# A token mixer on one core: pooling ahead of the attention, and six output projections split in two halves by their contraction

## The reference, cut to what matters

```python
def token_mixer(h, cos, sin, w_in, w_pool, pool_scale, sinks, g_pool, g_attn, w_out):
    z = h @ w_in
    u = z[..., :POOL_WIDTH]
    q = z[..., POOL_WIDTH:MIX_WIDTH].reshape(B, S, N_HEADS_2, HEAD_DIM_2)
    ...
    pool_out = pool_mix(u, w_pool, pool_scale)
    q = apply_partial_rope(q, cos, sin)
    k = apply_partial_rope(k, cos, sin)
    attn_out = swa_with_sinks(q, k, v, sinks)
    y = jnp.concatenate([rms_norm_2(pool_out, g_pool), rms_norm_2(attn_out, g_attn)], axis=-1)
    return y @ w_out
```

## Time and profile before

| | us |
|---|---|
| median of three executions | 2226.62 |
| lowest, highest | 2226.55, 2234.54 |
| the profiled execution, its whole time | 2232.97 |
| its span, first to last instruction | 2231.1 |
| TensorE busy in the span (97%) | 2171.8 |
| VectorE busy (56%) | 1258.4 |
| ScalarE busy (37%) | 819.9 |
| GpSimd busy (9%) | 194.2 |
| mean granted TensorE clock | 0.988 |

### The profile page before, as it was taken

One profiled execution on the slowest core, in us unless ns is written; L12 is line 12 of the kernel. 1 busy time (PEld: TensorE's weight loads), 2 busy tenths in 40 slices (PEclk: granted clock), 3 DMA queues, 4 the chain that ended last, 5 costly groups with the idle time before them and its releaser, 6 DMA issues.

```text
span 2231.1 us, 34854 instructions
## 1 busy us (share of the span) xinstructions
PE 2171.8 (97%) x14232; PEld 1811.3 (81%) x14232; DVE 1258.4 (56%) x1889; ACT 819.9 (37%) x1256; POOL 194.2 (9%) x142
## 2 busy tenths in 40 slices
PE   6999999999999999999999999999999899999998
PEld 5878788788888888888888888888897589888887
DVE  4789988898755555444533554443247735444423
ACT  4344433345454333223322542322233544322222
POOL 0100222103323001000000100000000210000000
PEclk9999999999999999999999999999999999999999
DMA  4242111122112243233332322333221112223321
GB/s 161 78 132 76 58 44 44 54 76 63 40 39 77 86 149 121 94 97 100 106 104 73 114 76 94 96 100 114 96 66 57 38 57 76 94 94 98 118 92 51
DMA packets 56170, 189.88 MB, mean 85 GB/s; under 512 B 6256, under 2 KB 8688, under 8 KB 56048
## 3 DMA queue, kind: packets, MB, share of 16 engines
q1 hardware_dynamic: 53168, 182.88, 25.3%
q10 hardware_dynamic: 2880, 5.24, 0.6%
HBM read 178.66 MB, written 9.44 MB: 84 GB/s over the span
## 4 chain that ended last, share of the span: by engine, by line
PE 81%; issue 10%; DVE 7%; ACT 2%; POOL 0%; DMA 0%; SPq 0%; ACTq 0%; DVEq 0%; POOLq 0%
PE pg L654 68%; PE pC L917 4%; PE pB L917 1%; DVE cpad L1883 1%; DVE sacc L2024 1%; DVE w_lo L1803 1%; PE pB L685 1%; ACT w_hi L1225 1%; PE pC L758 1%; PE pA L977 1%; PE pA L732 0%; PE pB L692 0%; PE pB L716 0%; PE pC L732 0%; DVE tb L2148 0%
## 5 line engine op out<-in xcount | busy, mean ns | idle before, releaser
L654 PE MATMUL pg<-a_hi,w_hi 128*128 128x512 f32 (+1 forms) x1920 | 747.2, 389 | 11.9 <-ACT ptile L1315 3.2
L654 PE MATMUL pg<-a_lo,w_hi 128*128 128x512 f32 (+1 forms) x1920 | 740.1, 385 | 0.0
L654 PE MATMUL pg<-a_hi,w_lo 128*128 128x512 f32 (+1 forms) x1920 | 737.8, 384 | 0.0
L1803 DVE TENSOR_TENSOR w_lo<-w_raw,w_hi 128x1024 fp32r<-128x1024 f32 (+3 forms) x299 | 382.6, 1280 | 395.3 <-ACT w_hi L1225 392.9
L1225 ACT ACTIVATE w_hi<-w_raw 128x1024 fp32r<-128x1024 f32 (+3 forms) x299 | 329.6, 1102 | 648.1 <-PE pg L654 637.1
L654 PEld LDWEIGHTS pg<-a_hi,w_hi 128*128 128x128 f32 x1920 | 362.7, 189 | 86.1 <-issue 8.0
L654 PEld LDWEIGHTS pg<-a_hi,w_lo 128*128 128x128 f32 x1920 | 362.8, 189 | 68.6 <-issue 1.6
L654 PEld LDWEIGHTS pg<-a_lo,w_hi 128*128 128x128 f32 x1920 | 362.9, 189 | 68.1 <-issue 0.9
L654 PE MATMUL pg<-h_hi,w_hi 128*128 128x512 f32 (+1 forms) x572 | 215.7, 377 | 0.6 <-DVE w_lo L1803 0.6
L654 PE MATMUL pg<-h_hi,w_lo 128*128 128x512 f32 (+1 forms) x572 | 214.5, 375 | 0.0
L654 PE MATMUL pg<-h_lo,w_hi 128*128 128x512 f32 (+1 forms) x572 | 212.4, 371 | 0.0
(11 more groups left out here) (359 smaller groups left out, 2346.7 us busy)
## 6 DMA issues: line engine op xcount, KB each, us to landing
w_raw<-in_w_gu SPq DMA_DIRECT2D x132, 512.0 KB, 3.5
w_raw<-in_w_in SPq DMA_DIRECT2D x74, 512.0 KB, 3.5
w_raw<-in_w_dn SPq DMA_DIRECT2D x48, 704.0 KB, 4.0
spill_g<-tmp ACTq DMA_DIRECT2D x16, 256.0 KB, 2.0
w_raw<-in_w_co SPq DMA_DIRECT2D x8, 512.0 KB, 3.6
w_raw<-in_w_do SPq DMA_DIRECT2D x8, 512.0 KB, 3.7
w_raw<-in_w_wo SPq DMA_DIRECT2D x8, 512.0 KB, 4.1
w_raw<-in_w_pg SPq DMA_DIRECT2D x8, 512.0 KB, 4.1
```

Source lines behind the costliest of these rows:

```text
L654: ins = pe.matmul(dst[:, cols], w_of(w, n % 2, k), b(k)[:, cols], start=first and q == 0, stop=last and q == len(todo) - 1)
L1803: dve.tensor_tensor(w_lo[:, n % 2, 0:c], w_raw[:, n % 4, 0:c], w_hi[:, n % 2, 0:c].bitcast(F32), ALU.subtract).then_inc(S("w_lo"), 1)
```

## The change

The weight of the six first output units is loaded in two halves: `mp` t, over the four pooling tiles, and `ma` t, over the four attention tiles, 12 products each. The mixer's input units stand in another order: `mu` 3 to 0 ahead of `mq` 0 and 1, all six whole ahead of the attention, with the four pooling matmuls between. The pooling part's norm (6) is summed in step 0 and spread in step 1; its factor goes to `tmp2`, its four tiles are scaled in steps 3 to 6 and their low parts taken in steps 7 to 10. Fillers are now `mq` 2 and 3 (8 products in each of three steps, none in steps 3 and 7), then `mp` 0 to 3: 3 products in each of steps 8 to 15, 8 in steps 16 to 18. `mp` 4 and 5 stand around the second norm (7). ScalarE copies an `mp` to `wd` or `up`; VectorE adds it to the `ma` of the same t on its way to `hb2`, ScalarE squares `hb2`. The factor `mix_post` moves from ScalarE's copy to VectorE's update of x. `mo` 6 and 7 stay whole.

```diff
@@ -315,3 +315,6 @@
-        MIX = [("mk", 0), ("mv", 0), ("mq", 0), ("mq", 1), ("mq", 2), ("mu", 3), ("mq", 3),
-               ("mu", 2), ("mu", 1), ("mu", 0)]
-        MFILL = MIX[5:]
+        MIX = [("mk", 0), ("mv", 0), ("mu", 3), ("mu", 2), ("mu", 1), ("mu", 0), ("mq", 0), ("mq", 1),
+               ("mq", 2), ("mq", 3)]
+        HALF_K = KT // 2
+        MFILL = [(("mq", 2), 3 * KT), (("mq", 3), 3 * KT)] + [(("mp", t), 3 * HALF_K) for t in range(4)]
+        MSTEP = [8, 8, 8, 0] * 2 + [3] * 8 + [8] * 3
+        assert sum(MSTEP) == sum(n for _, n in MFILL)
@@ -326 +329,4 @@
-        for i in range(KT):
+        for nm, k0 in (("mp", 0), ("ma", HALF_K)):
+            for i in range(KT - 2):
+                U.add((nm, i), a["w_out2"][i][:, k0 * P:(k0 + HALF_K) * P], HALF_K * P)
+        for i in range(KT - 2, KT):
...
+        MAUX = {3: 3, 7: 4}
+        YP = {("mu", 1): 3, ("mu", 0): 2, ("mq", 0): 1, ("mq", 1): 0}
+        for key in MIX:
@@ -399,4 +401,9 @@
-            for k in MAUX.get(3 * i + 2, []):
-                aux(k, "D" if k[0] == "rp" else "A")
-        aux(("yp", 0), "A")
-        for i in range(KT):
+            if key in YP:
+                aux(("yp", YP[key]), "A")
+            if key in (("mq", 2), ("mq", 3)):
+                aux(("rp", key[1] + 1), "D")
+        for i in range(KT - 2):
+            O.add(("mp", i), "A")
+        for i in range(KT - 2):
+            O.add(("ma", i), "D")
+        for i in range(KT - 2, KT):
...
+            def half_unit(key, k0, part=None):
+
+                n = U.at[key]
+                if part is None or part[0] == 0:
+                    pe.wait_ge(S("w_lo"), n + 1)
+                    begin(key)
+                ins = products(n, act_a(k0), HALF_K, bank(key), w_tile, part, ready=("a_lo", set_count("out", k0)))
+                if part is None or part[1] == 3 * HALF_K:
+                    ins.then_inc(S("gemm"), 1)
+
...
-            unit(("mq", 0))
-            unit(("mq", 1), part=(0, NORM_AT))
+            unit(("mu", 3), part=(0, NORM_AT))
@@ -1149,2 +1181,9 @@
-            unit(("mq", 1), part=(NORM_AT, UNIT))
-            unit(("mq", 2), part=(0, NORM_AT))
+            unit(("mu", 3), part=(NORM_AT, UNIT))
+            unit(("mu", 2))
+            unit(("mu", 1))
+            pooled(3)
+            unit(("mu", 0))
+            pooled(2)
+            unit(("mq", 0))
+            pooled(1)
+            unit(("mq", 1), part=(0, NORM_AT))
@@ -1152 +1191,2 @@
-            unit(("mq", 2), part=(NORM_AT, UNIT))
+            pooled(0)
+            unit(("mq", 1), part=(NORM_AT, UNIT))
...
@@ -1197,2 +1239,5 @@
-                if s < 15:
-                    unit(MFILL[s // 3], part=(s % 3 * UNIT // 3, (s % 3 + 1) * UNIT // 3))
+                for key, q, e, n in mixer_parts(s):
+                    if key[0] == "mq":
+                        unit(key, part=(q, e))
+                    else:
+                        half_unit(key, 0, (q, e))
@@ -1201,3 +1246,5 @@
-                for k in MAUX.get(s, []):
-                    (rotate if k[0] == "rp" else pooled)(k[1])
-            pooled(0)
+                    norm(6)
+                if s == 1:
+                    norm_out(6)
+                if s in MAUX:
+                    rotate(MAUX[s])
@@ -1205,2 +1252 @@
-            norm(6)
-            norm_out(6)
+            half_unit(("mp", 4), 0, (0, 8))
@@ -1207,0 +1254,2 @@
+            half_unit(("mp", 4), 0, (8, 12))
+            half_unit(("mp", 5), 0, (0, 4))
@@ -1208,0 +1257 @@
+            half_unit(("mp", 5), 0, (4, 12))
@@ -1210 +1259 @@
-                unit(("mo", t), ready=None if t else fresh("out"))
+                half_unit(("ma", t), HALF_K)
...
-            after(("mq", 1))
-            after(("mq", 2))
+            for key in MIX[2:8]:
+                if key == ("mq", 1):
+                    pooled(0)
+                after(key)
+                if key in YP and key != ("mq", 1):
+                    pooled(YP[key])
...
+            def pool_half(t):
+                after(("mp", t))
+                act.activation(pool_out(t), bank(("mp", t)), ACT.Copy).then_inc(S("evA"), 1)
+
+            def high_out(t):
+                act.wait_ge(S("mh"), t + 1)
+                act.activation(a_hi[:, t], mo[:, t], ACT.Copy).then_inc(S("a_hi"), 1)
@@ -1748,13 +1808,18 @@
-                if s < 15 and s % 3 == 2:
-                    after(MFILL[s // 3])
-                for k in MAUX.get(s, []):
-                    if k[0] == "yp":
-                        pooled(k[1])
-            pooled(0)
-            root(6)
-            for i in range(PT_):
-                act.wait_ge(S("oat"), i + 1)
-                square(7, i, mo[:, PT_ + i])
-            for t in range(PT_):
-                act.wait_ge(S("mh"), t + 1)
-                act.activation(a_hi[:, t], mo[:, t], ACT.Copy).then_inc(S("a_hi"), 1)
+                for key in mixer_done(s - 1) if s else []:
+                    if key[0] == "mp":
+                        pool_half(key[1])
+                    else:
+                        after(key)
+                if s == 0:
+                    root(6)
+                if 7 <= s < 7 + PT_:
+                    high_out(s - 7)
+                if s in (7, 11, 15):
+                    i = (s - 7) // 4
+                    act.wait_ge(S("oat"), i + 1)
+                    square(7, i, mo[:, PT_ + i])
+                if s == 15:
+                    act.activation(ost[:, 0:1], ost[:, 0:1], ACT.Sqrt)
+            act.wait_ge(S("oat"), PT_)
+            square(7, PT_ - 1, mo[:, KT - 1])
+            pool_half(3)
...
+            pool_half(4)
+            high_out(PT_)
+            high_out(PT_ + 1)
+            pool_half(5)
+            high_out(PT_ + 2)
+            high_out(PT_ + 3)
@@ -1766,4 +1834,3 @@
-                unit_out(act, ("mo", t))
-                full_square(2, t, bank(("mo", t)))
-                act.activation(hb2[:, t], bank(("mo", t)), ACT.Copy, scale=v("mix_post", t)).then_inc(S("evA"), 1)
-                after(("mo", t))
+                after(("ma", t))
+                ev_wait(act, ("ma", t))
+                full_square(2, t, hb2[:, t])
@@ -1774 +1841 @@
...
@@ -1841 +1908,2 @@
-                                ins = dve.scalar_tensor_tensor(y, src[:, t, TOK[h]], factor, y, ALU.mult, ALU.add)
+                                c = factor if isinstance(factor, float) else v(factor, t)
+                                ins = dve.scalar_tensor_tensor(y, src[:, t, TOK[h]], c, y, ALU.mult, ALU.add)
...
+            mixed(("mu", 3))
+            mixed(("mu", 2))
+            means(3)
+            mixed(("mu", 1))
+            means(2)
+            mixed(("mu", 0))
+            means(1)
+            mixed(("mq", 0))
+            means(0)
...
@@ -2493,10 +2573,14 @@
-                if s < 15 and s % 3 == 2:
-                    key = MFILL[s // 3]
-                    evac(key, zq[:, 1 + key[1]] if key[0] == "mq" else up[:, key[1], PW:])
-                if s % 3 == 0 and 0 < s < 16:
-                    after(MFILL[s // 3 - 1])
-                for k in MAUX.get(s, []):
-                    if k[0] == "rp":
-                        rotated(k[1])
-                if s in MEANS:
-                    means(MEANS[s])
+                for key in mixer_done(s - 1) if s else []:
+                    if key[0] == "mq":
+                        evac(key, zq[:, 1 + key[1]])
+                    after(key)
+                if s in MAUX:
+                    rotated(MAUX[s])
+                if s == 1:
+                    recip(6, (0,))
+                if s == 2:
+                    recip(6, (1,), dst=tmp2)
+                if 3 <= s < 3 + PT_:
+                    scaled_out(s - 3, 50, tmp2[:])
+                if 7 <= s < 7 + PT_:
+                    low("out", s - 7, mo[:, s - 7])
@@ -2507,8 +2591,11 @@
-            for nu, t0, at_ in ((6, 0, 50), (7, PT_, 54)):
-                recip(nu)
-                for t in range(t0, t0 + PT_):
-                    g = at_ + t - t0
-                    dve.scalar_tensor_tensor(mo[:, t], mo[:, t], gate_p[:, g:g + 1], rstd[:], ALU.mult, ALU.mult)\
-                        .then_inc(S("mh"), 1)
-                for t in range(t0, t0 + PT_):
-                    low("out", t, mo[:, t])
+            after(("mp", 3))
+            recip(7, (0,))
+            after(("mp", 4))
+            recip(7, (1,))
+            for t in range(PT_, KT + 1):
+                if t < KT:
+                    scaled_out(t, 50, rstd[:])
+                if t == PT_ + 2:
+                    after(("mp", 5))
+                if t > PT_:
+                    low("out", t - 1, mo[:, t - 1])
@@ -2516 +2603,3 @@
-                after(("mo", t))
+                unit_out(dve, ("ma", t))
+                dve.tensor_tensor(hb2[:, t], bank(("ma", t)), pool_out(t), ALU.add).then_inc(S("evD"), 1)
+                after(("ma", t))
@@ -2518 +2607 @@
-            new_x(2, hb2, 1.0, "ffn2_pre", {
```

(29 more changed lines are left out.)

52 lines of the change are left out of this document (23 added, 29 removed).

## The result

| | before | after |
|---|---|---|
| median of 11 executions, us | 2231.17 | 2239.38 |
| lowest, highest | 2226.55, 2238.08 | 2233.06, 2244.73 |
| span of the profiled execution | 2231.1 | 2235.8 |
| mean granted clock | 0.988 | 0.989 |

The ratio after to before is 1.0032, 95% interval 1.0018 to 1.0045: about 7 us slower (4 to 10). That is within 0.5%, the outcome that had a chance of 0.90, but the kernel got slower where 2 us less had been forecast. The three first executions of the kernel before had given 2226.62; with eight more its median is 2231.17. So the forecast time of 2224.6 was counted from a low start, and the sum is better judged by its difference: -2.0 forecast, +7.1 measured. The measured time lies above the range's high end of 2232. Counted from 2231.17 that end would be 2236.6, and 2239.38 lies above it too.

A forecast was written before the change was run, and what follows sets the result against it. VectorE and TensorE nearly fill the attention; TensorE is underused in the 20.06 us behind it. Terms 20.4 - 3.6 - 18.4 - 0.4 = -2.0 us, counted from 2226.62, gave 2224.6, range 2216 to 2232.

The forecast's parts named there:

- The part before the attention: From first whole projection to first mask addition: three more projections, four pooling matmuls and bank waits add 20.4 us.
- VectorE's own work in the attention: Up to the 15th division, VectorE's biases, divisions, rotations and other operations sum to 56.0 us and set the stretch.
- VectorE's waits: In the attention, 7.2 us of waits on top of VectorE's work give 63.2 against 66.76, so -3.6 us.
- The first norm's factor: Early in the attention, VectorE waits 2.9 us for the factor's spreading and for scores behind the norm's sums.
- Weight halves in pairs 3 and 7: In these pairs VectorE waits for a weight half that ScalarE converts behind the exponentials: 0.7 us each, 1.4 together.
- Late scores: In the attention, VectorE waits 0.7 us for the scores of pairs 5, 6 and 14.
- The half clock behind pauses: After TensorE's pauses in pairs 3 and 7, its lower clock costs VectorE 1.2 us, bounds nothing and 3.
- Behind the attention, -18.4: From the 15th division to the end of the sixth output, 54.8 us become 36.4, with 2.8 of low-part waits.
- Late part: After the sixth output: -0.6 us for TensorE's wait at the second late projection, +0.2 for factor columns, sum -0.4.
- The table loads: On ScalarE in the attention, two added function-table loads of 1.28 us each cost nothing, with 1.0 us to spare.
- The attention does not shrink: Rival: VectorE waits as before or a new chain holds it, attention 66.8 us, time 2228.2; chance 0.20.
- The clock rival: From pair 8 on, sparse TensorE work runs at 1.2 GHz, +2.4 us per pair, time 2234.2 to 2243.8; chance 0.10.

The follow-up runs named there:

- e2: The changed kernel with TensorE spreading the first norm's factor in step 2 instead of step 1: attention 66.10 us against 70.86, ratio to before 0.9997.
- e6: The changed kernel with the edits of e1, e2 and e3 together: attention 60.49 us against 70.86, ratio to before 1.0001.
- e1: The changed kernel with ScalarE writing the high parts ahead of the exponentials in steps 8 to 10: attention 63.56 us against 70.86, ratio to before 1.0009.
- e3: The changed kernel with TensorE computing its values seven times in steps 3 and 7, inside the pauses: attention 65.85 us against 70.86, ratio to before 1.0025.
- e5: The changed kernel itself, run again without an edit: attention 69.31 us against 70.86 the first time, ratio to before 1.0018.
- e4: The changed kernel with TensorE computing its values twice in steps 8 to 15: attention 70.30 us against 70.86, ratio to before 1.0016.
- e8: The changed kernel with e1, e2, no repeated values, and fillers and rotations moved so no matmul needs its own step's eviction: attention 59.20 us, ratio to before 0.9975.
- e7: e6 with VectorE's rotation ahead of the weight half, and in step 3 a scaling ahead of the rotation: attention 60.93 us, ratio to before 0.9985.

## Why the prediction was wrong

**The part before the attention, +20.4.** Right: +20.8.

**VectorE's own work in the attention, 56.0.** Right. The stretch less its waits (70.86 less 13.55) is 57.3, and 0.95 of that is one collision with GpSimd, a division of 1.57 in place of 0.62 beside a GpSimd addition of 1.27, for which I had 1.0 beside the 56.0. That leaves 56.4.

**VectorE's waits, 7.2: this is the step that failed.** They were 13.55, and the 7.2 had 1.0 for GpSimd in it, so 6.2 stands against 13.55.

- *The first norm's factor, 2.9.* 2.68: 0.57 + 2.11. e2 showed that half of it could have been avoided.
- *Weight halves in pairs 3 and 7, 1.4.* Right: 0.73 twice.
- *Late scores, 0.7.* The one of pair 6 was 0.68. Those of pairs 5 and 14, 0.76 and 0.70, are not there in e6 at full clock, so they stand under the half clock below.
- *The low parts of the pooling tiles, nothing.* Missing, and 3.69 by the rows; 4.0 by e1. I counted the four low parts as work of VectorE and asked nowhere who hands them their input. Behind the attention I did ask it. The kernel's order has the answer: on ScalarE `high_out(s - 7)` stands behind `prob(s)` and `pt_copy(s - 2)` of the same step in which VectorE takes the low part. ScalarE is idle 2.47 us ahead of the exponentials of steps 9 and 10, so the same work placed there is free.
- *The half clock behind pauses, 1.2 with bounds 0 and 3.* Too small. Behind the pauses of steps 3 and 7 it took 2.8 (e3), near the upper bound; behind the third pause, in steps 12 and 13, which I had not foreseen, 2.5 in the first trace and 1.0 in e5's. I gave pauses of pairs 3 and 7 "some 2.4 and 3", which were 2.27 and 2.80, so the place was right and the price not: behind a pause not just the transposes but the rotation's matmul, the next scores and values all ran at the low level.

In VectorE's rows the two make 3.69 and, for the clock, 0.80 + 0.69 + 0.76 + 1.65 + 0.70 = 4.60 less the 1.2 forecast: 7.1 of the 7.7 by which the attention is off. In the lengths of the steps it is 4.0 + (5.3 - 1.2) = 8.1. The rest is small terms of either sign.

**Behind the attention, -18.4.** Right within an us: -17.5. The spreading took 0.81 to the start of what follows (forecast 0.9) and the waits for low parts 2.36 (2.8); TensorE's busy time is 34.6, where the sum without these waits was 33.6.

**Late part, -0.4.** -0.9: from the end of the sixth output to the late sums 6.66 us in place of 7.58. TensorE doesn't wait at the second late projection any more. The factor column costs what was estimated, 478 ns for an update of x against 419. The four parts sum to 20.8 + 4.1 - 17.5 - 0.9 = +6.5, beside the mixer's 6.4.

**The table loads.** Hidden, as forecast. The Trainium skill's figure for a switch (ScalarE: Activation LUTs, "What ACT_TABLE_LOAD costs"), 2.66 us with a drain, isn't borne out for the path here: a row of 1.28, and the next operation 0.01 later.

**The rivals.** "The attention does not shrink" had the right direction and 0.20, but stopped at 66.8. The clock rival was right that the clock falls in this part and wrong about its cost. Three products per pair run at full clock where TensorE hardly waits (1786 to 1793 at 1.00; e6, all at 1.00). Behind the scattered waits of steps 8 to 10 the clock does fall in step 10, and e4's denser steps prevent that, as the rival would have it, but it costs no time there. What cost time was the low level behind the longer pauses. I held the two apart, one slow case with waits and one with the clock, and gave each alone; they came together. Of my three signs for being wrong, two were there: VectorE idle over 10 us, and a clock under 0.9.

**The answer to where the expected gain went.** Filling the idle 20 us behind the attention worked. It costs the same products ahead of the attention, so it is worth something only by what the attention gives up. The attention did get lighter: in e8, with the change's own work in it, it is 59.2 us, 7.6 less than before. As changed it gave all of that, and 4 us more, to VectorE's waits, for high parts and for a TensorE at half clock.

## What to carry to other kernels

When work is moved onto an engine as filler, list for each piece who makes its input in the same step, and where that stands in the other engine's order; a short piece behind a long one of the same step costs more than its own length. Put what has no input of this step at the head of the step, where the engine waits anyway. A pause of TensorE has to be priced with what runs behind it at the lower clock. And where a step has no filler, a matmul that needs an eviction of the same step makes two waits: TensorE's for the eviction (2.27 in step 3) and VectorE's for the matmul (0.80).

## What the runs showed that I had not expected

**The same pause, two clocks.** The pause of 1.83 us ahead of the transposes of step 12 stands in five traces of four kernels, with the same transposes behind it. In after and e5 they take 1.11 (in e4, with 1.84, 1.12), in e2 (and e3, with 1.84) 0.66. Here e5 and then e2:

```profile
1779.35 1.11 PE L1214 MATMUL pB<-consts,sm 128*128 128x128 f32 x4 [1.83 <-DVE sm L2558]
```

```profile
1774.34 0.66 PE L1214 MATMUL pB<-consts,sm 128*128 128x128 f32 x4 [1.83 <-DVE sm L2558]
```

**Two waits of 1.21 and 0.84 can do it.** Behind the attention TensorE waits 1.21 us for a low part, has three products, and waits 0.84 (in after 0.85) for the next. In after products of 0.50 and 0.40 us follow, in e5, the same program, eight of 0.57 to 0.80; in e8 the first one takes 0.62. The five us around the waits in e5 and in after:

```profile
1811.50:1816.50 5.00, 4.16 (x11) 2.66 (x11) 3.43 (x6) 1.70 (x4) 0.00 (x0) 0.68 0.17 52
```

```profile
1812.50:1817.50 5.00, 3.85 (x15) 2.38 (x15) 3.85 (x7) 2.04 (x5) 0.00 (x0) 1.00 0.16 52
```

The part from the 15th division to the late sums is 43.9 us in the four traces without this fall (after, e4, e6, e7) and 44.6 to 45.0 in the seven with it. The Trainium skill (TensorE: Matmul & The Clock Gate, "What's actually happening") says that how many matmuls run at the low level at a kernel's start varies from run to run of one kernel. After and e5 show such a difference in the middle of one. What in the execution decides it is not shown here. So a trace of one execution carries an uncertainty of some 1 us behind the attention and 1.5 us in it (70.86 and 69.31), and an edit's worth is to be read from the steps that it touches, in more than one trace.
